# Hawk/Conformer hybrid step on one core: one zero-padded product for the Conformer's sample taps, 14 prompt taps on TensorE, and the RG-LRU's squares and roots in another order

## The reference, cut to what matters

```
# layer 0, RG-LRU (recurrent mixer)
proj = xn @ w_in;  gate = gelu(proj[:, :1024]);  xr = proj[:, 1024:]
xc   = causal_depthwise(concat(conv_buf, xr), conv_w) + conv_b            # 4 taps
r, i = sigmoid(blockdiag(xc, w_a) + b_a), sigmoid(blockdiag(xc, w_i) + b_i)
a    = exp(-8 * r * softplus(-lam))
u    = sqrt(-expm1(2 * log a)) * (i * xc)                                 # log a is the exponent above
h[t] = a[t] * h[t-1] + u[t]
y    = (h * gate) @ w_out

# layer 1, Conformer convolution
p = xn @ w_pw1 + b_pw1;  z = p[:, :1024] * sigmoid(p[:, 1024:])
c = causal_depthwise(concat(conv_buf, z), dw_w) + dw_b                    # 31 taps per channel
c = silu(layernorm(c));  y = c @ w_pw2 + b_pw2
```

## Time and profile before

| what | value |
|---|---|
| median of 3 runs | 2303.93 us (2303.93 to 2304.86) |
| profiled execution: its time, its span | 2304.9 us, 2303.1 us |
| PE busy | 2218.6 us (96%) |
| DVE, ACT, POOL busy | 1700.1 us (74%), 1029.5 us (45%), 150.0 us (7%) |
| mean granted TensorE clock | 0.983 |

### The profile page before, as it was taken

How to read it: one execution, slowest core, us unless ns; L and a number is a source line. 1 busy time by engine, 2 the same in 40 slices (tenths; PEclk the granted TensorE clock), 3 DMA queues, 4 the chain that set the end, 5 groups by cost and what they waited for, 6 DMA issues and landing times.

```text
span 2303.1 us, 50784 instructions
## 1 busy us (share of the span) xinstructions
PE 2218.6 (96%) x21716; PEld 2182.7 (95%) x21716; DVE 1700.1 (74%) x3275; ACT 1029.5 (45%) x1513; POOL 150.0 (7%) x69
## 2 busy tenths in 40 slices
PE   7789999999999999999898899999999999999998
PEld 6789999999999999999897899999999999999998
DVE  7637998777558777886599279997775567768865
ACT  6644443344334434445575544533443344344443
POOL 2064000000000000000100550000000000000000
PEclk8899999999999999999999899999999999999999
DMA  5233543444444444445321474433444444444442
GB/s 184 90 133 118 182 150 128 138 150 154 147 147 147 147 144 141 138 138 200 120 83 46 113 154 153 159 130 129 156 149 155 143 151 147 142 144 138 135 160 94
DMA packets 99248, 321.22 MB, mean 139 GB/s; under 512 B 21328, under 2 KB 22480, under 8 KB 98768
## 3 DMA queue, kind: packets, MB, share of 16 engines
q1 hardware_dynamic: 89088, 314.69, 41.4%
q10 hardware_dynamic: 9936, 3.29, 0.7%
HBM read 315.50 MB, written 2.43 MB: 138 GB/s over the span
## 4 chain that ended last, share of the span: by engine, by line
PE 92%; DVE 6%; ACT 1%; issue 1%; DMA 0%; DVEq 0%; ACTq 0%
PE ps L690 28%; PE ps L692 27%; PE ps L691 26%; PE ps L748 8%; PE ps L759 2%; DVE work L918 1%; PE ps L675 1%; DVE w_lo L1150 1%; DVE rstd L912 1%; PE ps L800 0%; ACT w_hi L446 0%; DVE work L1055 0%; PE ps L771 0%; DVE hidden L1171 0%; DVE hidden L1162 0%
## 5 line engine op out<-in xcount | busy, mean ns | idle before, releaser
L690 PE MATMUL ps<-act_hi,w_hi 128*128 128x288 f32 x2688 | 816.6, 304 | 57.6 <-DVE act_lo L926 53.0
L691 PE MATMUL ps<-act_hi,w_lo 128*128 128x288 f32 x2688 | 800.0, 298 | 0.0
L692 PE MATMUL ps<-act_lo,w_hi 128*128 128x288 f32 x2688 | 798.1, 297 | 0.0
L1150 DVE TENSOR_TENSOR w_lo<-land,w_hi 128x1024 fp32r<-128x1024 f32 x532 | 650.5, 1223 | 170.0 <-ACT w_hi L446 169.2
L446 ACT CAST w_hi<-land 128x1024 fp32r<-128x1024 f32 x592 | 617.0, 1043 | 46.6 <-PE ps L692 44.1
L690 PE MATMUL ps<-g_hi,w_hi 128*128 128x288 f32 x2048 | 610.0, 298 | 4.4 <-DVE x L1300 4.4
L692 PE MATMUL ps<-g_lo,w_hi 128*128 128x288 f32 x2048 | 603.4, 295 | 0.0
L691 PE MATMUL ps<-g_hi,w_lo 128*128 128x288 f32 x2048 | 603.4, 295 | 0.0
L690 PEld LDWEIGHTS ps<-act_hi,w_hi 128*128 128x128 f32 x2688 | 511.2, 190 | 63.4 <-issue 56.3
L691 PEld LDWEIGHTS ps<-act_hi,w_lo 128*128 128x128 f32 x2688 | 512.2, 191 | 1.0
L692 PEld LDWEIGHTS ps<-act_lo,w_hi 128*128 128x128 f32 x2688 | 512.8, 191 | 0.0
(11 more groups left out here) (168 smaller groups left out, 1067.5 us busy)
## 6 DMA issues: line engine op xcount, KB each, us to landing
land<-stream_dram SPq DMA_DIRECT2D x592, 512.0 KB, 3.3
x<-x_dram SPq DMA_DIRECT2D x2, 576.0 KB, 4.5
y_t_dram<-work SPq DMA_DIRECT2D x8, 144.0 KB, 1.9
work<-keys_dram SPq DMA_DIRECT2D x1, 1024.0 KB, 7.6
work<-keys_dram ACTq DMA_DIRECT2D x1, 1024.0 KB, 5.4
work<-cstate_dram ACTq DMA_DIRECT2D x1, 960.0 KB, 7.8
cfs_t_dram<-hidden ACTq DMA_DIRECT2D x8, 120.0 KB, 12.4
work<-blocks_dram SPq DMA_DIRECT2D x4, 128.0 KB, 8.6
```

What stands on the lines that cost most here:

```text
L690: nc.tensor.matmul(out, w_hi[:, slot, wsl], hi, start=start, stop=False)
L691: nc.tensor.matmul(out, w_lo[:, slot, wsl], hi, start=False, stop=False)
L692: return nc.tensor.matmul(out, w_hi[:, slot, wsl], lo, start=False, stop=stop)
L1150: V.tensor_tensor(w_lo[:, k, :], land[:, k, :], w_hi[:, k, :].bitcast(F32), ALU.subtract).then_inc(lo_by_dve, 1)
```

## The change

Three things change.

1. RG-LRU: the squares of a half (`squares`) stand in VectorE's loop over the IN slabs, at `n` = 13 and 14, each ahead of that step's `split_lo`; the `split_lo` of slab OUT0 + 2 moves from between the two halves' squares to behind the first half's scan. ScalarE takes both roots at `n` = 14, and nothing at 15.
2. Conformer samples: the four products of 8 x 31 become one of 8 x 4 x 34: the row of 34 values of a sequence (30 of the state, 4 new) is multiplied by four rows of weights of 34, each row with the 31 taps shifted by its position and zeros around them. The sum is then over 34 values. GpSimd makes the rows (`wide_weights`: one memset, four copies) after slab 45 of layer 0 on its queue, when the V slabs of the experts whose place in `hidden` they take are used up.
3. Conformer prompt: TensorE does 14 taps for each chunk instead of 15, ScalarE taps 14 and 15, VectorE the other 15.

```diff
-SIDE_TAPS = 15
+SIDE_TAPS = 14
...
-        cv = view(flat, CH * ZEXT, CH, T)
+        wide_w = view(flat, CH * ZEXT, CH, SL, ZROW)
+        CV0 = CH * ZEXT + CH * SL * ZROW
+        cv = view(flat, CV0, CH, T)
...
-        conv_prod = view(work_f, E, NSEQ, SL, CF_W)
+        conv_prod = view(work_f, E, NSEQ, SL, ZROW)
...
+            def wide_weights():
+
+                pool.wait_ge(slab_used, max(r for r in V_AT if block_of(r) == 2) + 1)
+                pool.wait_ge(loaded, 16)
+                nc.gpsimd.memset(wide_w, 0.0).then_inc(wide_ready, 1)
+                pool.wait_ge(wide_ready, 1)
+                taps = cols[:, COLS["cf_dw_w"]:COLS["cf_dw_w"] + CF_W * CH].rearrange("p (k c) -> p c k", c=CH)
+                for t in range(SL):
+                    nc.gpsimd.tensor_copy(wide_w[:, :, t, t:t + CF_W], taps).then_inc(wide_ready, 1)
...
-                        if n in (14, 15):
-                            act.wait_ge(lru_dve, n - 13)
-                            part = u_g[:, 4 * (n - 14):4 * (n - 14) + 4, :]
-                            nc.scalar.activation(part, part, ACT.Sqrt).then_inc(lru_act, 1)
+                        if n == 14:
+                            for half in range(2):
+                                act.wait_ge(lru_dve, half + 1)
+                                part = u_g[:, 4 * half:4 * half + 4, :]
+                                nc.scalar.activation(part, part, ACT.Sqrt).then_inc(lru_act, 1)
...
+                def squares(half):
+                    h4 = slice(4 * half, 4 * half + 4)
+                    dve.wait_ge(lru_act, CH + 4 * (half + 1))
+                    did(V.tensor_tensor(tmp[:, h4, :], a_g[:, h4, :], a_g[:, h4, :], ALU.mult))
+                    settle()
+                    V.scalar_tensor_tensor(out=u_g[:, h4, :], in0=tmp[:, h4, :], scalar=1.0,
+                                           in1=u_g[:, h4, :], op0=ALU.add,
+                                           op1=ALU.mult).then_inc(lru_dve, 1)
+
                 for n in range(IN_N - 1):
+                    if n >= 13:
+                        squares(n - 13)
                     split_lo(IN0 + n + LEAD)
...
-                    for t in range(SL):
-                        did(V.tensor_tensor(conv_prod[:, :, t, :], seqs(zs)[:, :, t:t + CF_W],
-                                            wk.unsqueeze(1).to_broadcast([P, NSEQ, CF_W]), ALU.mult))
+                    shape = [P, NSEQ, SL, ZROW]
+                    did(V.tensor_tensor(conv_prod, seqs(z_ext[:, c, ZEXT_S:ZEXT]).unsqueeze(2).to_broadcast(shape),
+                                        wide_w[:, c, :, :].unsqueeze(1).to_broadcast(shape), ALU.mult))
...
+                dve.wait_ge(wide_ready, 1 + SL)
                 glu(0)
```

More of the change, by code:

```diff
@@ L201, in build @@
         z_ext = view(flat, 0, CH, ZEXT)
-        cv = view(flat, CH * ZEXT, CH, T)
[L203 to L207, removed]
+        wide_w = view(flat, CH * ZEXT, CH, SL, ZROW)
+        CV0 = CH * ZEXT + CH * SL * ZROW
+        cv = view(flat, CV0, CH, T)
+        sq_cf = view(flat, CV0 + CT, CH, T)
+        glu_gate = view(flat, CV0 + 2 * CT, 2, T)
+        pivot = view(flat, CV0 + 2 * CT + 2 * T, T)
+        mean = view(flat, CV0 + 2 * CT + 3 * T, T)
+        var = view(flat, CV0 + 2 * CT + 4 * T, T)
         Q_SLOT, TOP_SLOT, SCORE_SLOT = 16, 44, 48
@@ L311, in build @@
         glu_ready = sem("glu_ready")
+        wide_ready = sem("wide_ready")
         diag_ready = sem("diag_ready")
@@ L398, in _ @@
                                             ALU.subtract).then_inc(lo_by_pool, 1)
+                if n == POOL_END - 1:
+                    wide_weights()
         @block.scalar
@@ L982, in conv @@
                             settle()
+                tmp = r_h
+                def squares(half):
[6 more added lines that the diff above has]
+                                           op1=ALU.mult).then_inc(lru_dve, 1)
                 for n in range(IN_N - 1):
+                    if n >= 13:
+                        squares(n - 13)
                     split_lo(IN0 + n + LEAD)
@@ L997, in rg_mixer @@
                                   seqs(ext[:, c, EXT_S:EXT])[:, :, SL:]).then_inc(states_ready, 1)
[L999 to L1009, removed]
                 h0 = col("state_h", 0, 64).rearrange("p (c s) -> p c s", c=CH)
@@ L1028, in rg_mixer @@
                                              0.0, ALU.mult, ALU.add))
+                    if half == 0:
+                        split_lo(OUT0 + 2)
                     dve.wait_ge(gelu_ready, half + 1)
@@ L1061, in conv @@
                     dve.wait_ge(evacuated[1], USES + USE_IN + c + 1)
-                    wk = cols[:, COLS["cf_dw_w"]:COLS["cf_dw_w"] + CF_W * CH].rearrange(
-                        "p (k c) -> p c k", c=CH)[:, c, :]
-                    zs = z_ext[:, c, ZEXT_S:ZEXT]
-                    for t in range(SL):
-                        did(V.tensor_tensor(conv_prod[:, :, t, :], seqs(zs)[:, :, t:t + CF_W],
-                                            wk.unsqueeze(1).to_broadcast([P, NSEQ, CF_W]), ALU.mult))
+                    shape = [P, NSEQ, SL, ZROW]
+                    did(V.tensor_tensor(conv_prod, seqs(z_ext[:, c, ZEXT_S:ZEXT]).unsqueeze(2).to_broadcast(shape),
+                                        wide_w[:, c, :, :].unsqueeze(1).to_broadcast(shape), ALU.mult))
                     products = steps[0]
```

## The result

| kernel | median us (runs) | ratio to before, 95% |
|---|---|---|
| before | 2303.93 (2303.73 to 2304.86, 4) | |
| changed | 2291.31 (2290.49 to 2294.93, 4) | 0.9947 [0.993, 0.9965] |

What follows compares the result with a forecast made beforehand. TensorE was taken as the bound (92% of the chain), so only its work or waits count; -5.0 (RG-LRU), -2.6 and -0.8 (Conformer) and 0 (GpSimd) gave -8.4 us, 2303.9 to 2295.5, range 2293.2 to 2299.0.

Steps and rivals of the forecast that it cites:

- RG-LRU, -5.0: RG-LRU ahead of OUT: reordering VectorE's queue starts the product with the Gelu gate at 93.11 instead of 98.12, -5.0 us.
- the sum: Whole kernel: the work terms -5.0, -2.6 and -0.8 added from start-to-start prices in the profile, -8.4 us.
- Gelu's cover: RG-LRU: Gelu's first half on ScalarE ends by 91.3, 1.8 us before VectorE wants it, hiding ScalarE's part.
- Conformer, -2.6 and -0.8: Conformer: six TensorE chunks each 0.43 us shorter, -2.6; the last two `conv` on VectorE each 0.38 shorter, -0.8.
- The product's price: Conformer, VectorE: the wide product of 1088 elements takes 1.21 us, where the four products took 2.09.
- both rivals on it: Wide product: at the four's rate, 2.00 us, total 2300.7 (8%); or far worse, at 3.1 us total 2309.5 (3%).
- GpSimd, 0: GpSimd's memset and four copies near 1038: at most 5.0 us, covered by its idle gap, so 0.
- The second rival: Near 1038: GpSimd's work blocks VectorE, 0.83 us lost for each us, TensorE loses up to 3.1; total 2297.1 (9%).
- The clock, "about 1.5 either way for the four": Four TensorE restarts behind the changed places: shifting against the clock spreads the time about 1.5 us either way.

Runs made afterwards that it cites:

- `again`: The changed kernel run once more, unaltered, against the kernel before; 2291.09 us (0.9946).
- `rg_only`: The kernel before with the RG-LRU part of the change alone; 2294.53 us (0.9961).
- `lo18`: The kernel before with only the split of slab OUT0 + 2 moved behind the first scan and both roots at step 14; 2298.61 us (0.9976).
- `after_p17`: The changed kernel with one more VectorE multiply of 1568 elements, result unused, ahead of the first half's carry; 2297.93 us.
- `warm2_before`: The kernel before with matmuls of constants, result unused, filling TensorE's waits (mended placement); 2288.16 us (0.9932).
- `warm2_after`: The changed kernel with matmuls of constants, result unused, filling TensorE's waits (mended placement); 2279.41 us (0.9893).

## Why the prediction was right and wrong

- **RG-LRU, -5.0: right, -5.2 measured.** Each start is where the sum put it, counted from the exponentials, but for the product with the Gelu gate, which comes 0.2 us earlier; Gelu's cover was 2.3 us, not 1.8. By the profiles all of it is the moved squares and splits; the roots' move, which the sum needed only for Gelu's cover, is worth 0.
- **Conformer, -2.6 and -0.8: right.** Chunk 12.44, wait 0.21, last two `conv` 0.8 shorter. The product's price was the forecast's, 1.20 from start to start, and both rivals on it fell. By the rule of the Trainium skill that the prediction weighed ("Vector Engine (DVE) Microarchitecture Reference", 5.2), rows of adjacent words that start on an 8-byte boundary run at the full rate. The trace now agrees, 1088 elements in 1.28 us beside 1.22 for a `w_lo` of 1024.
- **GpSimd, 0: right, by its cover.** Its work was 5.3 us, not at most 5.0: a copy of 248 elements took 1.07 us where 0.6 was counted. The second rival's effect is there (VectorE lost 0.8 us beside 4.28 us of copies), but at a fraction of its price of 0.83 for each us of GpSimd, and it stayed in VectorE's idle time.
- **The clock, "about 1.5 either way for the four": the step that failed.** The mechanism was named and the price of a us at the low level was right (about half, 0.445 measured). The term was mis-sized: it gave four restarts together no more than the 1.5 us of one, for which no row spoke, and took it as a spread to both sides. With the clock held up the change is worth 8.75 us where the median moved by 12.6, so the clock gave 3.9, all one way.

  First, a restart does not come alone: where it is dear, the wait of 2.31 us some 87 us behind it lets the clock fall again, which the sum did not list, so the first stretch of the table has two prices some 2.2 us apart, the last one 2.9. Second, it is not only a lot drawn anew in each execution: the executions of one kernel do differ (`again` against the first profile), but the median too moves with the length of the RG-LRU stretch, by more than that length in `rg_only`, `lo18` and `after_p17`.

  Between the profiles of before and of `again`, 12.6 us apart, the parts are 8.6 of work, 2.5 in the stretch from Q of layer 0, 1.1 in when the first restart came (22.98 and 21.85) and 0.4 elsewhere. That before pays the dear price more often and the changed kernel the cheap one is inferred from their medians, since only single executions have a trace; what is shown is that with the clock held up the two are 8.75 apart, and the sum was 8.4.

The Trainium skill ("TensorE: Matmul & The Clock Gate", Part 1: The HAM clock gate) says that how much runs at the low rate behind a start varies from run to run and costs less than 1% of a span. The runs agree in size (0.68% between before and `warm2_before`) and in that it varies (997.93 and 995.39 us for one stretch of the same kernel). They also show a part that goes with the kernel and stays in the median.

What stays open: why a given length of the stretch gives the dear or the cheap price. The multiplies added on the path show that it is no steady function (6.8, 6.3 and 8.8 us above the changed kernel for 1.8, 3.7 and 5.6 us of work), not by what rule it goes.

## What to carry to other kernels

Sum the work of a change from the rows, but when TensorE restarts after waits, a shift of a few us re-deals the clock at the later restarts and at short waits behind them, and the median can move with it by as much as a small change is worth (here 3.9 us beside 8.75): a change of 0.2% can't be judged by the time alone there. Hold the clock up in both kernels (matmuls of constants in the waits) and compare those: the spread fell from 6.2 us to about 1, the difference came out within 0.4 us of the forecast sum, and the filling itself was worth 0.68%, more than the change; both together, 2279.41 us, are 1.1% below before.

Where two engines are level in a loop, as here TensorE and VectorE in the Conformer, relieve both in one change: each half alone left the loop at the other engine's pace (12.87 and 12.94 us for a chunk, 12.44 with both).

## What the runs showed of the hardware that was not expected

- Matmuls of constants kept the granted clock at 0.999 over the whole program in `warm2_before` and `warm2_after`, with 4 to 29 of them in a wait; with up to 1.4 us left idle ahead of a restart (1.42 at OUT of `warm2_before`) it stayed at the full level.
- A wait of 2.31 us in the middle of steady work let the clock fall for 3.4 us in one execution of the changed kernel (the first profile) and not in another (`again`).
- GpSimd's copies of 248 elements to the shifted rows took 1.07 us each (4.28 for 4), as long as its memset of 1088 (1.01).
